# A two-block model on one core: eight more buffers for the modulation weights in S5, y read back by another queue, and three norms whose row factor is applied when a product is read out

## The chip, the cores and the metric

The kernel runs on one core of a Trainium2 chip. The metric is the device time of one execution in microseconds (us), lower is better. The core has five engines that run their own instruction streams and meet at semaphores: PE (TensorE, matmuls), DVE (VectorE), ACT (ScalarE), POOL (GpSimd) and SP (SyncE, here only transfers). ACT and POOL can start transfers too.

## The reference

```python
# first block (512 tokens and 16 meta tokens, width 1024)
n = _rmsnorm(h, g_mix[layer])
proj = n @ w_in[layer]
...
y_ssd = _ssd_mixer(xbc, dt_raw, z, dt_bias[layer], a_log[layer], d_ssd[layer], g_ssd[layer])
y_s5 = _s5_mixer(u, lam_re[layer], lam_im[layer], log_step[layer], ...)
mix = jnp.concatenate([y_ssd.astype(h.dtype), y_s5.astype(h.dtype)], axis=-1)
h = h + mix @ w_out[layer]
m = _rmsnorm(h, g_mlp[layer]) @ w_up[layer]
h = h + jnp.square(jax.nn.relu(m)) @ w_down[layer]
# _ssd_mixer ends with _rmsnorm(y * silu(z), g_norm)
# _s5_mixer ends with _rmsnorm(v[..., :D_S5] * jax.nn.sigmoid(v[..., D_S5:]), g_norm), v = gelu(y) @ w_glu + b_glu
# _rmsnorm(x, g): x * rsqrt(mean(x * x, axis=-1) + 1e-5) * g
```

A second block of two layers follows (convolution, windowed attention, gated merge, convolutional FFN, each modulated by `silu(c) @ w_ada + b_ada`). The change does not touch its code. Only its modulation weights matter here: the kernel computes `silu(c) @ w_ada` piece by piece inside the first block.

## The kernel before, in words

Activations lie transposed: 128 channels on the partitions, tokens along the row, eight tiles of 128 channels. Each fp32 product is made of three products of fp32r halves (hi of the weights by hi of the input, hi by lo, lo by hi). A **unit** is the 128 output channels of one weight tile of 512 KB: 24 matmuls of 512 columns. Its raw weights land in one of R = 4 slots of `wraw`; ACT copies them to `whi` (`split_hi`, L237), POOL subtracts to get `wlo` (`split_lo`, L245), PE multiplies into PSUM bank s, and ACT or DVE reads the bank out and frees it (`acc_free`). Slot s is split again for unit g + 4 as soon as unit g is done. The first four units of a matrix run interleaved as a **quad** (`pe_quad`, L314), so that they can start while the input tiles still come one by one; the others run one after another (`pe_unit`, L284).

The stages in order of time, with their places in the program:

- SSD (`ssd_pe`, `ssd_dve`, `ssd_act`): four chunks of 128 tokens. Its squares are summed over channels by one-column matmuls (`ssd_sums_pe`, L805).
- A norm before a product: ACT squares each tile, DVE adds the squares up (`norm_add`, L412), PE sums over partitions (L446), ACT takes the root, DVE the reciprocal, PE spreads the row over all partitions (`norm_rows_pe`, L454), DVE scales each tile by gain and row factor (L498), ACT rounds it to hi (L437), DVE subtracts to get lo (L508). PE's first matmul of the next quad waits for all that. It happens after SSD, after GLU (norm "s5") and after the second output product (norm "mlp").
- OUT1 (units U_OUT1, eight), added to `res` by `add_unit_dve` (L1022).
- S5: eight passes. In a pass i DVE scans the states (`s5_scan`) and makes tables for pass i + 2 (`s5_tables`), PE forms states and output (`s5_w_pe`, `s5_y_pe`, L1354, L1367, L1375), ACT applies gelu, writes y to memory in eight transfers (L1452), moves the kernel tile in eight more (`s5_move`, L1425) and rounds the y that came back (`s5_hi`, L1429). SP reads y back in another layout (`s5_y_back`, L1239). Between these PE computes the modulation (`ada_pe`, L664), eight tiles of `w_ada` a pass; the tiles land in the four `wraw` slots, so SP can be four ahead, and SP issues in program order: a wait of y's way back holds the weight loads behind it.
- GLU (16 units), OUT2 (8 units), then the MLP: four chunks c, each with 8 up units and 8 down units. For up unit m ACT takes the relu out of PSUM (`rl`, L1524), splits the weights of the unit four later (L237), and rounds the square to `hhi` (L1529); DVE squares (`rv`, L1554) and subtracts (`hlo`, L1556). In the last chunk ACT and DVE also do the squares of the context's norm (L401, L412).

Of the kernel before, what the change touches and what calls it, by code (L numbers as in the profile page):

```python
# [24 lines left out]
P = 128  # L25
# [39 lines left out]
U_ADA = U_GLU + R  # L65
# [54 lines left out]
def build(nc, A, out, ud, yd, pd):  # L120
# [18 lines left out]
    wlo = at("wlo", [P, R, 8, P], 32 * K, F32R)  # L139
    O_H, O_HC, O_X = 48 * K, 64 * K, 72 * K  # L140
# [45 lines left out]
    acc_free = [sem(f"acc_free{s}") for s in range(R)]  # L186
    s_in = [sem(f"inputs_landed{h}") for h in range(4)]
# [119 lines left out]
    def pe_quad(pe, g, i, rb, xh, xl, T, nk=8, hi=None, lo=None, wide=False, c0=0, more=None, between=None, held=None):  # L307
# [347 lines left out]
    def ada_pe(pe, first, last):  # L655

        for u in range(first, last):
            a, j = divmod(u, 12)
            s, rnd = ada_slot(u)
            pe.wait_ge(landed[s], (rnd + 1) * 16)  # L660
            w = wraw[:, s].rearrange("p (k a) m -> p k (a m)", k=2)
# [147 lines left out]
    def ssd_pe(pe):  # L809
# [36 lines left out]
        for c in (NCH - 2, NCH - 1):  # L846
            ssd_sums_pe(pe, c)
# [30 lines left out]
    def ssd_square_act(act, c):  # L878
# [3 lines left out]
        else:  # L882
            act.wait_ge(d_gd.sem, d_gd.past("g"))
        act.activation(xbc[:, 0:NT, chunk(c)], Y[:, :, chunk(c - 1)], ACT.Square).then_inc(d_sq.sem, 1)

    def ssd_act(act):
# [17 lines left out]
        ada_cols(act, 2)  # L904
        ssd_square_act(act, NCH - 1)
# [63 lines left out]
    def ssd_dve(dve):  # L969
# [32 lines left out]
        for g in range(2):  # L1002
# [99 lines left out]
    s_yr = [sem(f"s5_y_landed{b}") for b in range(2)]  # L1102
# [324 lines left out]
    def s5_hi(act, i):  # L1427
        act.wait_ge(s_yr[i % 2], 16 * (i // 2 + 1))
        act.activation(hhi[:, i], yf[:, i % 2], ACT.Copy).then_inc(f_h.sem, 1)  # L1429

    def s5_act(act):
# [4 lines left out]
        for i in range(NT):  # L1436
            if i + 1 < NT:
                s5_move(act, i + 1)
            if i in ADA_END:
                ada_rows(act, ADA_END[i])  # L1440
            if i:
# [7 lines left out]
            if i >= 2:  # L1449
                act.wait_ge(s_yr[i % 2], 16 * (i // 2))  # L1450
# [11 lines left out]
    def glu_act(act):  # L1462
# [4 lines left out]
        for m in range(NT):  # L1467
# [7 lines left out]
            if m:  # L1475
                norm_square(act, n, m - 1, src, SEQ, out_done)
# [1381 lines left out]
```

## Time and profile before

| | |
|---|---|
| median of 3 runs | 3154.59 us (3140.21 to 3154.74) |
| the profiled execution | 3153.16 us |
| its span, first to last instruction | 3151.4 us |
| PE busy | 2870.8 us, 91% of the span |
| DVE busy | 1604.7 us, 51% |
| POOL busy | 1266.5 us, 40% |
| ACT busy | 1086.8 us, 34% |
| mean granted clock of TensorE | 0.958 of full speed |

The span is the profiler's, the time around it is 1.8 us more. Busy times are averages over stages with different limits; what a change is worth is read in its own stage.

### The profile page before, as it was taken

To read this page: it belongs to the slowest core of one execution; us is meant where nothing else is said; L and a number is where in the kernel's file an instruction comes from. 1 tells how busy PE (TensorE), PEld (TensorE's weight loads), DVE (VectorE), ACT (ScalarE), POOL (GpSimd) and SP (SyncE) were. 2 spreads that over 40 slices of the span, in tenths; PEclk is the share of its full clock that TensorE was granted. 3 is DMA by queue.
4 is the path that set the end of the run, shared out by engine and by line. 5 is a ranking of instruction groups with operands and counts; after the bars stand their busy time and mean duration, and the time that the engine had idled before them with its cause. 6 is when DMAs were issued, how large, how long until landed. Compare 5 with 4: busy or idle time off the path is not lost.

```text
span 3151.4 us, 41933 instructions
## 1 busy us (share of the span) xinstructions
PE 2870.8 (91%) x15576; PEld 2323.1 (74%) x15576; DVE 1604.7 (51%) x2055; ACT 1086.8 (34%) x1593; POOL 1266.5 (40%) x689
## 2 busy tenths in 40 slices
PE   6999877989998998988878999999988989799997
PEld 6975634778777887766667888888876767687786
DVE  6864674353334254388854422313246976552424
ACT  4534222323223232235433522313242453253332
POOL 3442200424434181486632322222337773434443
PEclk9989898989999999999989999999989999899999
DMA  5226587323223233422121112111222211222221
GB/s 174 91 80 214 169 251 222 100 74 95 93 79 107 81 121 120 147 76 72 61 67 60 67 60 64 63 61 60 74 81 97 71 61 62 93 80 94 93 92 69
DMA packets 116017, 306.80 MB, mean 97 GB/s; under 512 B 36128, under 2 KB 44448, under 8 KB 115232
## 3 DMA queue, kind: packets, MB, share of 16 engines
q1 hardware_dynamic: 87008, 286.06, 27.8%
q10 hardware_dynamic: 28864, 18.76, 2.2%
q8 instruction: 97, 1.59, 0.2%
q14 instruction: 48, 0.39, 0.0%
HBM read 294.95 MB, written 7.45 MB: 96 GB/s over the span
## 4 chain that ended last, share of the span: by engine, by line
PE 72%; DVE 13%; DVEq 5%; ACT 3%; DMA 2%; issue 2%; ACTq 1%; SPq 1%; POOL 0%; POOLq 0%
PE ps L284 35%; PE ps L314 18%; PE ps L305 6%; DVE co L2043 4%; PE ps L1751 2%; DVEq L2044 2%; PE ps L2154 2%; PE ps L664 1%; DMA wraw<-w_ada 1%; DVE sm L2019 1%; DVE pex L2028 1%; DMA wraw<-stream 1%; DVE mv L2233 1%; PE ps L1755 1%; PE ps L1756 1%
## 5 line engine op out<-in xcount | busy, mean ns | idle before, releaser
L245 POOL TENSOR_TENSOR wlo<-wraw,whi 128x1024 fp32r<-128x1024 f32 x373 | 925.6, 2490 | 1707.5 <-ACT whi L237 1706.0
L237 ACT ACTIVATE whi<-wraw 128x1024 fp32r<-128x1024 f32 x373 | 392.6, 1055 | 554.4 <-PE ps L314 174.5
L284 PE MATMUL ps<-xhi,whi 128*128 128x512 f32 (+1 forms) x1328 | 469.8, 370 | 1.7 <-issue 1.7
L284 PE MATMUL ps<-xlo,whi 128*128 128x512 f32 (+1 forms) x1328 | 470.6, 371 | 0.0
L284 PE MATMUL ps<-xhi,wlo 128*128 128x512 f32 (+1 forms) x1328 | 334.0, 371 | 0.0
L284 PEld LDWEIGHTS ps<-xhi,whi 128*128 128x128 f32 x1328 | 240.5, 188 | 48.1 <-issue 2.7
L284 PEld LDWEIGHTS ps<-xlo,whi 128*128 128x128 f32 x1328 | 240.5, 188 | 44.5
L284 PEld LDWEIGHTS ps<-xhi,wlo 128*128 128x128 f32 x1328 | 232.3, 188 | 44.8
L2043 DVE SCALAR_TENSOR_TENSOR co<-ub,vec,co 128x512 f32<-128x512 f32 (+1 forms) x216 | 251.7, 1205 | 5.4 <-issue 0.4
L1024 DVE SCALAR_TENSOR_TENSOR res<-ps,mod,res 128x512 f32 (+1 forms) x64 | 47.6, 748 | 260.0 <-PE ps L305 151.4
L2140 POOL TENSOR_TENSOR co<-co,ct 128x512 f32<-128x512 f32 (+1 forms) x144 | 164.0, 1139 | 20.7 <-issue 0.4
L284 PE MATMUL ps<-hhi,whi 128*128 128x512 f32 x408 | 159.2, 390 | 2.0 <-DVE gt L2227 1.8
L284 PE MATMUL ps<-hlo,whi 128*128 128x512 f32 x408 | 158.8, 389 | 0.0
L1755 PE MATMUL ps<-xhi,whi 128*128 128x512 f32 x352 | 144.5, 411 | 5.1 <-DVE ub L2055 3.5
L2138 POOL TENSOR_TENSOR ct<-ub,vec 128x512 f32<-128x512 f32 (+1 forms) x144 | 137.0, 951 | 22.9 <-issue 12.6
L2372 DVE SCALAR_TENSOR_TENSOR f<-ps,vec,f 128x511 f32<-128x511 f32 x88 | 50.2, 612 | 176.2 <-ACT f L2344 176.2
L1756 PE MATMUL ps<-xlo,whi 128*128 128x512 f32 x352 | 139.0, 395 | 0.0
L664 PE MATMUL ps<-wraw,cs 128*2 128x512 f32 x384 | 91.3, 620 | 28.8 <-DMA wraw<-w_ada 28.7
L1022 DVE TENSOR_TENSOR res<-res,ps 128x512 f32<-128x512 f32 x48 | 32.7, 687 | 164.4 <-PE ps L314 89.3
L305 PE MATMUL ps<-xchi,whi 128*128 128x256 f32 x352 | 100.5, 286 | 7.3 <-POOL wlo L245 7.3
L314 PE MATMUL ps<-xhi,whi 128*128 128x512 f32 (+1 forms) x320 | 96.5, 402 | 10.3 <-ACT xhi L437 8.8
L314 PE MATMUL ps<-hhi,whi 128*128 128x512 f32 x280 | 91.8, 418 | 14.7 <-DVE fa L2376 6.7
(390 smaller groups left out, 5723.7 us busy)
## 6 DMA issues: line engine op xcount, KB each, us to landing
wraw<-stream SPq DMA_DIRECT2D x425, 512.0 KB, 3.4
wraw<-w_ada SPq DMA_DIRECT2D x96, 512.0 KB, 4.9
biasb<-attn_bias ACTq DMA_DIRECT2D x32, 256.0 KB, 3.2
xin<-x0T SPq DMA_DIRECT2D x4, 528.0 KB, 6.9
s_u<-uk ACTq DMA_DIRECT2D x8, 264.0 KB, 3.4
res<-x0T ACTq DMA_DIRECT2D x1, 2048.0 KB, 8.6
s_y<-yk ACTq DMA_DIRECT2D x64, 32.0 KB, 4.4
yf<-s_y SPq DMA_DIRECT2D x8, 256.0 KB, 2.9
```

Of the source, the lines that this page charges most:

```text
L237: act.activation(whi[:, s], wraw[:, s], ACT.Copy).then_inc(hi_done[s], 1)
L245: pool.tensor_tensor(wlo[:, s], wraw[:, s], whi[:, s].bitcast(F32), ALU.subtract).then_inc(lo_done[s], 1)
L284: last = pe.matmul(ps[:, bank, 0:b - a], w[:, s, kt], x[:, kt, c0 + a:c0 + b], start=start, stop=stop)
L305: return pe.matmul(ps[:, R + s, 0:CTX], w[:, s, kt], part[:, kt], start=start, stop=stop)
L314: last = pe.matmul(ps[:, bank, 0:b - a], w[:, s, kt], x[:, kt, c0 + a:c0 + b], start=start, stop=stop)
L664: ins = pe.matmul(ps[32 * part + 32:32 * part + 34, ada_bank(a), :], cs[:, kt], w[:, h], start=kt == 0, stop=kt == 7)
L1751: last = pe.matmul(o, wraw[:, s, kt], x1[:, kt, 0:p.T], start=kt == 0, stop=kt == NT - 1)
L1755: pe.matmul(o, whi[:, s, kt], xhi[:, kt, 0:p.T], start=kt == 0, stop=False)
L1756: pe.matmul(o, whi[:, s, kt], xlo[:, kt, 0:p.T], start=False, stop=False)
L2043: dve.scalar_tensor_tensor(o, ub[:, m, k:k + p.T], colr(f"dw{p.l}", 1, k * 4 + m), o, ALU.mult, ALU.add)
L2138: pool.tensor_tensor(ct[:, 0:T], ub[:, m, k:k + T], colr(f"dw{l}", 1, k * 4 + m).to_broadcast([P, T]), ALU.mult)
L2140: ins = pool.tensor_tensor(o, o, ct[:, 0:T], ALU.add)
```

## The change

**Buffers.** While S5 runs, `whi` and `wlo` are free. The change lays eight slots `wada` over them, for the modulation tiles from number 40 on, with semaphores of their own; the first round waits for the last OUT1 units. The raw weights of OUT1's second half are loaded before S5's tables instead of after, and those of GLU inside S5, split at its end. **y back** is issued by POOL's queue for passes 0 to 6. **Norms** "ssd", "s5" and "mlp": ACT rounds `src * gain` straight to hi, DVE makes lo, and the row factor multiplies the product when it is read out of PSUM. The sums and the spreading of the row move into the quad. **MLP**: the row factor and the relu are one DVE operation out of PSUM, and ACT squares.

```diff
+RA = 8
+    wada = at("wada", [P, RA, 8, P], 16 * K)
+        if u >= ADA_RAW:
+            return (u - ADA_RAW) % RA, (u - ADA_RAW) // RA
...
         for kt in range(tail):
+            if early and kt == 3:
+                early()
             if hi is not None:
                 hi(pe, kt)
...
+        if between:
+            between()
         for j in range(R):
             product(j, wlo, xh, tail - 1)
...
+    def raw_hi_act(act, n, kt, src, g, dst):
+        act.activation(dst[:, kt, 0:SEQ], src(kt), ACT.Copy, scale=g(kt)).then_inc(n_hi.sem, 1)
+    def raw_row_dve(dve, n):
+        r = norm_row_dve(dve, n, SEQ)
+        dve.tensor_copy(nrs[:, 0:SEQ], r)
+        dve.drain()
+        return nrs[:, 0:SEQ]
+    def raw_lo_dve(dve, n, kt, src, g, hi, lo):
+        dve.wait_ge(n_hi.sem, n_hi.past("hi", hi_before[n] + kt))
+        dve.scalar_tensor_tensor(lo[:, kt, 0:SEQ], src(kt), g(kt), hi[:, kt, 0:SEQ].bitcast(F32), ALU.mult, ALU.subtract).then_inc(n_lo.sem, 1)
...
-        pe.wait_ge(d_wm.sem, d_wm.past("wm", 2 * (NCH - 2)))
-        for c in (1, 2):
-            ssd_sums_pe(pe, c)
         for g in range(2):
             ssd_y_pe(pe, NCH - 1, g)
         ada_turn(pe, 2)
-        for c in (NCH - 2, NCH - 1):
-            ssd_sums_pe(pe, c)
...
+        if r is not None:
+            dve.tensor_tensor(ps[:, s, 0:T], ps[:, s, 0:T], r, ALU.mult)
+            dve.drain()
         d = dst[:, m, 0:T]
...
+            if i == NT - 1:
+                for g in range(U_GLU, U_GLU + R):
+                    split_hi(act, g)
             if i:
                 s5_hi(act, i - 1)
...
+    def out2_act(act):
+        n = NORM["mlp"]
+        added = lambda e, kt: e.wait_ge(acc_free[(U_OUT2 + kt) % R], read_out(U_OUT2 + kt))
+        for m in range(NT):
+            split_hi(act, U_OUT2 + m + R)
+            if m:
+                norm_square(act, n, m - 1, rsrc, SEQ, added)
+        s, rnd = slot(U_OUT2 + NT - 1)
+        act.wait_ge(unit_done[s], rnd + 2)
+        for kt in range(NT):
+            added(act, kt)
+            raw_hi_act(act, n, kt, rsrc, g1("g_mlp"), xhi)
...
+    def raw_pe(pe, U, n, xh, xl, sums):
+        pe_quad(pe, U, 0, 0, xh, xl, SEQ, early=sums, between=lambda: norm_rows_pe(pe, NORM[n], SEQ), **normed(n))
...
# mlp_act, up unit m
-                act.wait_ge(unit_done[s], rnd + 2)
-                act.wait_ge(m_v.sem, m_v.past("v", c * 8 + m, 2))
-                ins = act.activation(rl[:, m % 2], ps[:, s, :], ACT.Relu)
-                ins.then_inc(acc_free[s], 1)
+                act.wait_ge(acc_free[(U_FF + m) % R], read_out(U_FF + m, c, 4))
+                act.wait_ge(m_l.sem, m_l.past("lo", c * 8 + m, 2))
+                act.activation(rv[:, m % 2], rl[:, m % 2], ACT.Square).then_inc(m_v.sem, 1)
                 split_hi(act, U_FF + m + R, c, 4)
                 act.wait_ge(m_v.sem, m_v.past("v", c * 8 + m))
                 act.activation(hhi[:, m], rv[:, m % 2], ACT.Copy).then_inc(m_h.sem, 1)
...
# mlp_dve, up unit m
-                dve.wait_ge(acc_free[(U_FF + m) % R], read_out(U_FF + m, c, 4))
-                dve.wait_ge(m_h.sem, m_h.past("hi", c * 8 + m, 2))
-                dve.tensor_tensor(rv[:, m % 2], rl[:, m % 2], rl[:, m % 2], ALU.mult).then_inc(m_v.sem, 1)
+                dve.wait_ge(unit_done[s], rnd + 2)
+                dve.wait_ge(m_v.sem, m_v.past("v", c * 8 + m, 2))
+                dve.scalar_tensor_tensor(rl[:, m % 2], ps[:, s, :], 0.0, r, ALU.max, ALU.mult).then_inc(acc_free[s], 1)
                 dve.wait_ge(m_h.sem, m_h.past("hi", c * 8 + m))
                 dve.tensor_tensor(hlo[:, m], rv[:, m % 2], hhi[:, m].bitcast(F32), ALU.subtract).then_inc(m_l.sem, 1)
-                if c is LAST:
-                    norm_add(dve, first, m, CTX)
+                for kt in (2 * m, 2 * m + 1) if c is LAST and m < 4 else ():
+                    norm_add(dve, first, kt, CTX)
...
# SP
+            segment(U_OUT1 + R, U_OUT1 + R, R)
...
             for i in range(NT):
                 a = ADA_SSD + ADA_HEAD + 8 * i
                 for j in range(8):
                     if i + 1 < NT:
                         load_ada(a + j)
-                    if j == 1 and i:
-                        s5_y_back(sp, i - 1)
                     if j == 3 and i + 2 < NT:
                         s5_load(sp, i + 2)
+                if i == NT - 3:
+                    segment(U_GLU, U_GLU, R)
             s5_y_back(sp, NT - 1)
...
# POOL
-            pool_units(pool, U_OUT1, 2)
+            pool_units(pool, U_OUT1, 1)
+            for i in range(NT - 1):
+                s5_y_back(pool, i)
+            for g in range(U_GLU, U_GLU + R):
+                split_lo(pool, g)
```

How the order moves at two places. First DVE at the start of the MLP. Before:

```order
L508 SCALAR_TENSOR_TENSOR xlo<-ntt,xhi 128x512 [waits norm_hi] x2
...
L1554 TENSOR_TENSOR rv<-rl 128x512 [waits mlp_hi]
L1555 REGISTER_ALU
L1556 TENSOR_TENSOR hlo<-rv,hhi 128x512 [waits mlp_hi]
L1553 REGISTER_ALU [waits acc_free2]
L1554 TENSOR_TENSOR rv<-rl 128x512 [waits mlp_hi]
```

and now:

```order
L468 SCALAR_TENSOR_TENSOR xlo<-res,vec,xhi 128x512 [waits norm_hi] x8
L427 TENSOR_TENSOR nacc<-nacc,nsq 128x512 [waits norm_square]
L501 RECIPROCAL nst<-nst 128x4 [waits norm_root]
L461 COPY nrs<-ps 128x512 [waits norm_row]
...
L1649 SCALAR_TENSOR_TENSOR rl<-ps,nrs 128x512 [waits mlp_square]
L1650 REGISTER_ALU
L1651 TENSOR_TENSOR hlo<-rv,hhi 128x512 [waits mlp_hi]
L1648 REGISTER_ALU [waits unit_done2]
L1649 SCALAR_TENSOR_TENSOR rl<-ps,nrs 128x512 [waits mlp_square]
```

The reading of a bank (`rl` out of `ps`) now stands on DVE, between the subtraction of one unit and that of the next; before, it was ACT's.

Second SP's transfers in one S5 pass. Before:

```order
L2486 DMA wraw<-w_ada 128x1024 [waits w_lo1]
L2486 DMA wraw<-w_ada 128x1024 [waits w_lo2]
L1239 DMA yf<-s_y 128x512 [waits s5_y_written1]
L2486 DMA wraw<-w_ada 128x1024 [waits w_lo3]
L2486 DMA wraw<-w_ada 128x1024 [waits w_lo0]
L1232 DMA u3a<-s_u 16x8x66 [waits s5_output]
```

and now:

```order
L2590 DMA wada<-w_ada 128x1024 [waits ada_used0]
L2590 DMA wada<-w_ada 128x1024 [waits ada_used1]
L2590 DMA wada<-w_ada 128x1024 [waits ada_used2]
L2590 DMA wada<-w_ada 128x1024 [waits ada_used3]
L1270 DMA u3a<-s_u 16x8x66 [waits s5_output]
L1270 DMA u3a<-s_u 16x8x66 x7
L2590 DMA wada<-w_ada 128x1024 [waits ada_used4]
```

The load of y (`yf`) is gone from SP, and a weight load waits for a slot used eight tiles ago (`ada_used`), not four (`w_lo`).

## Rows read from the trace of the kernel before

**Rows 1.** The page, part 4: the chain that ended last, by engine

```profile
PE 72%; DVE 13%; DVEq 5%; ACT 3%; DMA 2%; issue 2%; ACTq 1%; SPq 1%; POOL 0%; POOLq 0%
```

**Rows 2.** Chain of waits, 600 to 830 us: start us, us, what

```profile
599.81 26.08 PE ps L284 x115
...
633.79 2.09 PE ps L454 x8
...
637.37 25.26 PE ps L314 x96
662.63 22.14 PE ps L284 x96
...
695.93 25.02 PE ps L314 x96
...
744.70 21.39 PE ps L314 x93
```

**Rows 3.** Windows: busy of PE, PEld, DVE, ACT, POOL; clock, DMA share, GB/s

```profile
400.00:524.00 124.00, 95.34 (x1288) 46.28 (x1285) 86.74 (x145) 32.09 (x53) 0.00 (x0) 0.92 0.94 269
...
638.00:644.00 6.00, 6.00 (x17) 4.72 (x16) 5.54 (x10) 2.69 (x5) 0.00 (x0) 0.54 0.00 0
```

**Rows 4.** Timeline of ACT, first MLP chunk: start us, us, line, operation, tiles

```profile
716.22 0.60 ACT L1524 ACTIVATE rl<-ps 128x512 f32<-128x512 f32 x1 [11.04 <-PE ps L314]
716.72 1.05 ACT L237 ACTIVATE whi<-wraw 128x1024 fp32r<-128x1024 f32 x1
717.69 0.63 ACT L1529 ACTIVATE hhi<-rv 128x512 fp32r<-128x512 f32 x1
...
743.60 1.05 ACT L237 ACTIVATE whi<-wraw 128x1024 fp32r<-128x1024 f32 x1
```

**Rows 5.** Timeline of DVE, first MLP chunk

```profile
742.83 2.10 DVE L1556 TENSOR_TENSOR hlo<-rv,hhi 128x512 fp32r<-128x512 f32 x1 [0.70 <-ACT hhi L1529]
...
762.95 0.69 DVE L1022 TENSOR_TENSOR res<-res,ps 128x512 f32<-128x512 f32 x1 [0.90 <-PE ps L314]
```

**Rows 6.** Timeline of POOL, first MLP chunk

```profile
741.71 2.67 POOL L245 TENSOR_TENSOR wlo<-wraw,whi 128x1024 fp32r<-128x1024 f32 x1 [2.72 <-ACT whi L237]
...
762.56 9.48 POOL L245 TENSOR_TENSOR wlo<-wraw,whi 128x1024 fp32r<-128x1024 f32 x4 [15.37 <-ACT whi L237]
```

**Rows 7.** The page, part 5: a product with one PSUM source on DVE

```profile
L1024 DVE SCALAR_TENSOR_TENSOR res<-ps,mod,res 128x512 f32 (+1 forms) x64 | 47.6, 748 | 260.0 <-PE ps L305 151.4
```

**Rows 8.** Timeline of ACT, last MLP chunk, first unit read

```profile
985.64 0.60 ACT L1524 ACTIVATE rl<-ps 128x512 f32<-128x512 f32 x1 [17.03 <-PE ps L314]
```

**Rows 9.** Chain of waits, 0 to 1600 us: norm after SSD, last down quad

```profile
320.53 2.09 PE ps L454 x8
324.11 24.59 PE ps L314 x96
...
1021.91 23.77 PE ps L314 x96
```

**Rows 10.** Waits, 374 to 532 us: who for whom, us in total, times, longest

```profile
PE ps L1334 <- DVE res L1022: 4.2, 1, 4.2
```

**Rows 11.** Timeline of PE in S5, passes 0 and 6

```profile
397.19 1.16 PE L1367 MATMUL ps<-spv,cab 64*64 64x64 f32 x64
...
513.00 1.16 PE L1367 MATMUL ps<-spv,cab 64*64 64x64 f32 x64
```

**Rows 12.** Timeline of ACT in S5

```profile
455.14 5.42 ACTq L1425 DMA_DIRECT2D mt<-ka  x8
...
471.20 5.79 ACTq L1425 DMA_DIRECT2D mt<-ka  x8
...
478.99 0.63 ACT L1429 ACTIVATE hhi<-yf 128x512 fp32r<-128x512 f32 x1
```

**Rows 13.** Timeline of SP in S5: y read back

```profile
471.77 0.33 SPq L1239 DMA_DIRECT2D yf<-s_y  x1
```

**Rows 14.** The page, part 6: y's way back, us to landing

```profile
yf<-s_y SPq DMA_DIRECT2D x8, 256.0 KB, 2.9
```

More of the change, by code:

```diff
@@ L186, in build @@
     acc_free = [sem(f"acc_free{s}") for s in range(R)]
+    ada_landed = [sem(f"ada_landed{s}") for s in range(RA)]
+    ada_used = [sem(f"ada_used{s}") for s in range(RA)]
     s_in = [sem(f"inputs_landed{h}") for h in range(4)]
@@ L196, in raw_round @@
     def raw_round(g, i=0, rb=0):
-        return slot(g, i, rb)[1] + (N_ADA // R if g >= U_ADA else ADA_SSD // R if g >= U_OUT1 + R else 0)
+        return slot(g, i, rb)[1] + (ADA_RAW // R if g >= U_GLU else ADA_SSD // R if g >= U_OUT1 + R else 0)
     def whole(g):
@@ L212, in ada_slot, with ada_worked @@
     def ada_slot(u):
-        return slot(U_ADA + u if u >= ADA_SSD else U_OUT1 + R + u)
+        if u >= ADA_RAW:
+            return (u - ADA_RAW) % RA, (u - ADA_RAW) // RA
+        return slot(U_GLU + u if u >= ADA_SSD else U_OUT1 + R + u)
+    def ada_worked(eng, u):
+        s, rnd = ada_slot(u)
+        eng.wait_ge((lo_done if u < ADA_RAW else ada_used)[s], rnd + 1)
     def loop(eng, n, body):
@@ L305, in second, with pe_quad @@
         return pe.matmul(ps[:, R + s, 0:CTX], w[:, s, kt], part[:, kt], start=start, stop=stop)
-    def pe_quad(pe, g, i, rb, xh, xl, T, nk=8, hi=None, lo=None, wide=False, c0=0, more=None, between=None, held=None):
+    def pe_quad(pe, g, i, rb, xh, xl, T, nk=8, hi=None, lo=None, wide=False, c0=0, more=None, between=None, held=None, early=None):
         tail = nk - 2
@@ L516, in build @@
             "c1a": 9, "l1a": 10, "l1b": 11, "final2": 12}
-    hi_before, lo_before, done, kept_lo = [], [], 0, 0
+    RAW = ("ssd", "s5", "mlp")
+    hi_before, lo_before, t_before, done, kept_lo, scaled_done = [], [], [], 0, 0, 0
     for name in NORM:
+        t_before.append(scaled_done)
+        scaled_done += 0 if "final" in name or name in RAW else NT
         hi_before.append(done)
@@ L804, in ssd_sums_pe @@
         for kt in range(NT):
-            last = pe.matmul(ps[:, 0, c - 1:c], xbc[:, kt, chunk(c)], ones[:, 0:1], start=kt == 0, stop=kt == NT - 1)
+            last = pe.matmul(ps[:, 4, c - 1:c], xbc[:, kt, chunk(c)], ones[:, 0:1], start=kt == 0, stop=kt == NT - 1)
         if c == NCH - 1:
@@ L1005, in ssd_dve @@
             y = Y[:, 4 * g:4 * g + 4, chunk(c - 1)]
-            ins = dve.tensor_tensor(y, y, zs[:, 4 * g:4 * g + 4, chunk(c - 1)], ALU.mult)
-        ins.then_inc(d_gd.sem, 1)
+            dve.tensor_tensor(y, y, zs[:, 4 * g:4 * g + 4, chunk(c - 1)], ALU.mult).then_inc(d_gd.sem, 1)
         dve.drain()
+        for kt in range(NT):
+            raw_lo_dve(dve, NORM["ssd"], kt, ysrc, g1("g_ssd"), hhi, hlo)
     ysrc = lambda kt: Y[:, kt]
@@ L1101, in build @@
     s_yw = [sem(f"s5_y_written{b}") for b in range(2)]
-    s_yr = [sem(f"s5_y_landed{b}") for b in range(2)]
+    s_yr = [sem(f"s5_y_landed{i}") for i in range(NT)]
     e_pa, e_pv = steps("s5_param_scalar", "step", "mag", "sin"), steps("s5_param_vector", "ls", "angle", "kept")
@@ L1558, in chunk @@
                     dve.drain()
-                if c is LAST:
-                    norm_add(dve, first, m, CTX)
+                for kt in (2 * m, 2 * m + 1) if c is LAST and m < 4 else ():
+                    norm_add(dve, first, kt, CTX)
             if c is not LAST:
@@ L2498, in _ @@
                 s5_load(sp, i)
-            segment(U_OUT1 + R, U_OUT1 + R, U_ADA - U_OUT1 - R)
-            for u in range(ADA_SSD, ADA_SSD + ADA_HEAD):
+            for u in range(ADA_SSD, ADA_RAW):
                 load_ada(u)
@@ L2531, in _ @@
             ssd_pe(pe)
[L2532 to L2533 removed]
+            raw_pe(pe, U_OUT1, "ssd", hhi, hlo, lambda: raw_sums_ssd(pe))
             s5_pe(pe)
```

141 lines of the change are left out of this document (90 added, 51 removed).

## Prediction

> **What bounds the kernel now.** I read the page first, then the chain of waits, then the timelines of the stages that the change touches. PE holds 72% of the chain [rows 1], so a change counts where it moves PE's next matmul. In the chain PE stands still at each norm: GLU's last matmul ends at 625.9, the row is spread at 633.8, OUT2's quad starts at 637.4 and ends at 662.6 [rows 2]; OUT2 ends at 684.8, the MLP's quad runs from 695.9 to 720.95 [rows 2]. [...] So a quad after a stop takes 25.3 or 25.0 us, while 93 matmuls took 21.4 at 744.7 [rows 2], which is 22.1 for 96: the stop costs another 3.1 us. In S5 the passes take (513.00 - 397.19) / 6 = 19.3 us [rows 11] with the DMA engines 0.94 busy [rows 3]. In the MLP almost nothing is idle: the down quad starts at 744.7, 0.05 us after ACT's split of the last weights ended at 744.65 [rows 2, 4].
>
> **The change, part by part.** Negative is time won, in the profiled execution.
>
> *Norm after SSD.* The sums of the squares move behind the last products, into the quad. PE's work is the same, only short gaps go, such as the 1.5 us from 322.6 to 324.1 [rows 9]; the long row of one-column sums now lies inside the quad, where the clock may fall again. Nothing to -5 (the gap, another like it, and the quad's 24.6 against 22.1) [rows 9]; I take -2.
>
> *Before S5.* PE waited 4.2 us for DVE, which had tables to make ahead of the last adds [rows 10]. POOL now splits only four units there instead of eight, so the tables are done early; left is the last bank's read, now a product and an add of 0.69 each, 1.5 with the hand-over [rows 5]. 1.5 - 4.2 = -2.7, between -4 and -1.
>
> *S5.* Two floors. ACT's own work of a pass, with no one late, took 471.20 - 455.14 = 16.1 us [rows 12]. The transfers: 124 us at a share of 0.94 are 117 us of work over 124 / 19.3 = 6.4 passes, so 18.1 us a pass [rows 3, 11], less what the eight added slots bring in before pass 0. GLU's four tiles come in on top. I take 17.3, so 6 x (17.3 - 19.3) = -12; the ends are 16.1 (-19) and 19.3 (0). y back by POOL's queue has no row. y's way back starts at 471.77 and lands 2.9 later, and ACT uses it at 478.99 [rows 12 to 14]: it may come 4.3 us later at no cost. Its own price I take as nothing, its ends are nothing and the rival below. Its gain is that SP's loads no longer queue behind it, which is in the 17.3.
>
> *End of S5.* ACT splits GLU's four units just before the last pass: 4 x 1.05 = 4.2 us [rows 4], mostly while it waits for PE. POOL's four need 4 x 2.4 [rows 6] and end before the quad wants them. Nothing to +4; I take +1.
>
> *Norm "s5".* PE can start the quad when GLU's last two banks are read (a sigmoid like the relu's 0.60 [rows 4] and a strided product, longer than 0.75 [rows 7]): some 2 us after 625.9, of which the first matmuls fill 0.5. Then 22.1 for the quad and, inside it, sums and row, 2.1 each at most at half clock [rows 2], say 3 together. 1.5 + 22.1 + 3 = 26.6 against 662.6 - 625.9 = 36.7: -10. Should the clock still fall, -7; at best -12.
>
> *Norm "mlp".* ACT may write `xhi` only after OUT2's last unit: its split 1.05, a square, a hi of 0.63 [rows 4], 2.3 us. The first lo needs DVE, whose add of squares is held by POOL's split (see below) until 1.05 + 2.67 + 0.55 = 4.3, then 0.7: about 5 us [rows 4 to 6], of which four matmuls fill 1. So 4 + 22.1 + 3 + 3.1 for the clock = 32.2 against 36.2 [rows 2]: -4, between -8 and -1.
>
> *The MLP's chunks.* This is the large term. DVE now reads the bank, waits for ACT's square, split and hi, subtracts, and only then reads the next bank. One round: read 0.75 [rows 7], to the split 0.50, to hi 0.97, hi 0.63 [rows 4], hand-overs 0.1: the subtraction starts at 2.95. ACT's split ended at 2.35 and POOL's started. The trace shows what that does: the subtraction at 742.83 ran into POOL's 741.71 to 744.38 and ended at 744.93, 0.55 after it [rows 5, 6]; the add out of PSUM at 762.95 ran in 0.69 beside POOL's row from 762.56 [rows 5, 6]. So operations with both sources in SBUF wait for POOL's end, those out of PSUM do not. POOL ends at 2.4 + 2.4 to 2.67, the subtraction at about 5.5: one unit costs 5.5 us. The four units of the quad finish 1.6 apart and the others 5.5 apart (22.14 / 4 [rows 2]), so the lag of the quad is never made up: unit 7 is read 7 x 5.5 = 38.5 after unit 0, and its weights' slot is split 2.4 later, at 716.2 + 40.9 = 757.1 against 744.65 before [rows 4]. PE's down quad cannot bring in its fourth unit before that: +12.4, and 3.1 for the clock after the stop. Three chunks: +46.5. In the last one the adds of the context's squares come two a unit in the first four, some 0.85 us a unit more (two of half the width of 0.69, with their drain): 4 x 6.35 + 3 x 5.5 + 2.4 = 44.3 after 985.6 [rows 8] is 1029.9 against 1021.9 [rows 9]: +8, and the quad 25.1 instead of 23.8: +9.3. Together +55.8. The alternative reading of the same row is that the subtraction takes a fixed 2.1 us beside POOL, so 5.1 a unit: 3 x (9.6 + 3.1) + 6.5 = +44.6. I take the first and keep 44 and 65 as ends.
>
> [...]
>
> Sum: -2 - 2.7 - 12 + 1 - 10 - 4 + 55.8 = **+26**. 3153.2 + 26 = **3179 us**. The profiled execution stands 1.4 us under the median of the runs, so that against the median it is +25, 0.8% slower.
>
> **The rivals.**
>
> *The MLP's chain is quick enough.* If nothing holds DVE's subtraction, a unit costs 2.95 + 0.69 = 3.65, unit 7 is read on time (7 x 3.65 = 25.6, PE needs 26.9), and the last chunk even wins some 5. Then -30 - 5: 3118 us. For it: ACT's square relieves DVE of one held operation of the two. Against: POOL's split starts before the subtraction in every unit. The point is 3.8 us a unit; above it, PE waits. Chance 0.12.
>
> *The chain costs less than I say*: 5.1 a unit, 3168 us, within no change. For it: the rows of 2.1. Against: the ends tied to POOL's. Chance 0.13.
>
> *S5 wins nothing.* y comes back more than 4.3 us late through POOL's queue and ACT waits for it ahead of the gelu, or the DMA engines are the limit at 19.3 after all. In front of y's use DVE runs its tables; if POOL cannot issue during them (12 operations of about 0.69 each [rows 5], some 8 us, less the 4.3 of slack), y is 4 late and the pass is 16.1 + 4 = 20. Then +38 to +42: 3191 to 3195. Against: POOL has nothing else to do in S5. [...] Chance 0.15.
>
> **How the numbers follow.** My own case has 0.60 and, with its ends (44 to 65 for the MLP, the smaller terms partly offset), runs from 3165 to 3200. The range 3140 to 3202 takes in the middle rival and the S5 rival and leaves out the fast one (0.12) and a tail above. A measurement of this kernel can tell some 0.5%, 15.8 us, from no change: 3139 to 3170. Faster: the first rival and a sliver, 0.13. Within: the second rival and the low end of my case, 0.17. Slower: 0.70.
>
> **What would show it.** Right: in every MLP chunk about 12 us between the last up unit and the main part of the down quad, with PE waiting for ACT's `whi`; the subtraction of `hlo` near 2.4 us and starting 5.5 apart; half clock at the start of the down quads; S5 passes near 17.3; OUT2's quad starting within 2 us of GLU's end. Wrong: up units read 4 us apart or less, no idle PE before the down quads, or S5 passes of 19 and more with ACT waiting for y.

## Result and profile after

| | before | after |
|---|---|---|
| median | 3147.7 us (6 runs, 3140.21 to 3154.74) | 3174.27 us (6 runs, 3166.6 to 3180.37) |
| ratio | | 1.0085, 95% interval 1.007 to 1.010 |
| profiled execution | 3153.16 us | 3171.6 us |
| its span | 3151.4 us | 3169.8 us |
| mean granted clock | 0.958 | 0.955 |

The change costs 26.6 us by the medians and 18.4 us between the two spans. The forecast was 3179 us, slower. In the page's chain, PE's share has fallen from 72% to 68% and "issue" has risen from 2% to 7% [rows 1]:

```profile
PE 68%; DVE 14%; issue 7%; DVEq 5%; ACT 3%; DMA 1%; ACTq 1%; POOL 0%; SPq 0%; POOLq 0%
```

The chain of waits of after, 600 to 830 us (start, length, what), answers to [rows 2]:

```profile
612.92 7.16 PE ps L325 x30
620.09 0.79 PE ps L477 x8
620.87 8.46 PE ps L325 x36
629.33 0.89 PE ps L485 x8
630.22 6.47 PE ps L325 x28
636.69 22.14 PE ps L295 x96
...
660.59 2.38 DVE nacc L427
663.06 0.76 DVE xlo L468
663.87 8.92 PE ps L325 x28
...
706.35 0.70 DVE rl L1649
...
723.47 1.05 ACT whi L248
724.56 23.96 PE ps L325 x93
748.52 21.77 PE ps L295 x96
771.43 16.95 PE ps L325 x72
```

To read the losses and gains, take the same event in both traces and follow the difference from one to the next. GLU's end: 625.9 before, 610.8 now, so 15 us are won up to there. OUT2's quad ends at 636.69 instead of 662.63: 25.9 won. It starts 2.1 us after GLU's end and its sums (0.79) and row (0.89) stand inside it. The MLP's first quad ends at 689.4 instead of 720.95: 31.6 won, the most there ever is. From there it is lost again. The first down quad's main part starts at 724.56 instead of 744.70 (20.1 won), and so on through four chunks, until behind the last down quad the changed kernel is 14.7 us late. The second block gives the other 3.6 us: its code is the same, and one of its operations took 1247 ns on average instead of 1205 (L2138, 216 times, 9.1 us in all), and what sets that is open. Of the eleven runs below six have 1233 to 1247 ns there and five 1200 to 1214, so up to 10 us of DVE's work in a single trace belong to no change under test.

Where the MLP loses can be seen on DVE and POOL. Timelines of after, 700 to 722 us, DVE and then POOL:

```profile
698.46 2.48 DVE L1651 TENSOR_TENSOR hlo<-rv,hhi 128x512 fp32r<-128x512 f32 x1 [2.17 <-ACT hhi L1621]
700.86 0.68 DVE L1649 SCALAR_TENSOR_TENSOR rl<-ps,nrs 128x512 f32<-128x512 f32 x1
703.71 2.48 DVE L1651 TENSOR_TENSOR hlo<-rv,hhi 128x512 fp32r<-128x512 f32 x1 [2.17 <-ACT hhi L1621]
706.35 0.69 DVE L1649 SCALAR_TENSOR_TENSOR rl<-ps,nrs 128x512 f32<-128x512 f32 x1 [0.16 <-issue]
```

```profile
697.98 2.41 POOL L256 TENSOR_TENSOR wlo<-wraw,whi 128x1024 fp32r<-128x1024 f32 x1 [3.09 <-ACT whi L248]
703.23 2.40 POOL L256 TENSOR_TENSOR wlo<-wraw,whi 128x1024 fp32r<-128x1024 f32 x1 [2.84 <-ACT whi L248]
```

Each subtraction of `hlo` starts 0.47 or 0.48 us after POOL's split has begun and ends 0.54 to 0.56 us after the split has ended (703.23 + 2.40 = 705.63, 703.71 + 2.48 = 706.19). The next bank is read after it. The page has all 32 of them:

```profile
L1651 DVE TENSOR_TENSOR hlo<-rv,hhi 128x512 fp32r<-128x512 f32 x32 | 78.6, 2457 | 69.8 <-ACT hhi L1621 69.8
```

In the first chunk the banks are read at 684.69 and, seven units on, at 722.22: 5.36 us a unit. From the end of its first up unit to that of its last PE computes for only 26.9 us of the 37.5, so it stands still before the down quad and then begins it at a granted clock of 0.50. Windows of after (busy of PE, PEld, DVE, ACT, POOL; clock, DMA share, GB/s):

```profile
724.00:728.00 4.00, 3.44 (x8) 2.76 (x9) 2.44 (x1) 1.03 (x2) 2.36 (x1) 0.50 0.21 85
728.00:740.00 12.00, 12.00 (x50) 9.76 (x50) 0.00 (x0) 0.00 (x0) 0.00 (x0) 0.91 0.13 44
```

In S5 the passes took (494.89 - 387.25) / 6 = 17.9 us instead of 19.3 [rows 11]; the timeline of PE in passes 0 and 6:

```profile
387.25 1.16 PE L1405 MATMUL ps<-spv,cab 64*64 64x64 f32 x64
...
494.89 1.16 PE L1405 MATMUL ps<-spv,cab 64*64 64x64 f32 x64 [0.59 <-DVE spv L1341]
```

A new wait appears there. In the waits, 370 to 530 us, PE hardly waits for modulation weights any more, but ACT waits for y (us in all, times, longest):

```profile
ACT hhi L1467 <- DMA yf<-s_y: 32.0, 5, 11.9
...
PE ps L701 <- DMA wada<-w_ada: 1.2, 2, 0.8
```

Of the same window before, the rows are

```profile
PE ps L664 <- DMA wraw<-w_ada: 26.1, 18, 3.4
...
ACT hhi L1429 <- DMA yf<-s_y: 1.9, 1, 1.9
```

### The profile page after: what moved, and what is told of

The parts are those of the page before. It is cut to its first block, busy times and chain, and to the rows that moved or that the text cites. A ratio compares the mean times of both kernels' runs of the same rounds, so it can differ in the third digit from the quotient of the medians.

```text
span 3169.8 us, 41861 instructions
## 1 busy us (share of the span) xinstructions
PE 2866.9 (90%) x15576; PEld 2317.3 (73%) x15576; DVE 1596.6 (50%) x2050; ACT 1086.1 (34%) x1593; POOL 1260.2 (40%) x696
## 4 chain that ended last, share of the span: by engine, by line
PE 68%; DVE 14%; issue 7%; DVEq 5%; ACT 3%; DMA 1%; ACTq 1%; POOL 0%; SPq 0%; POOLq 0%
PE ps L295 34%; PE ps L325 17%; PE ps L316 6%; DVE co L2138 4%; PE ps L1846 2%; DVEq L2139 2%; PE ps L2249 2%; DVE sm L2114 1%; DVE hlo L1651 1%; DVE mv L2328 1%; DMA wraw<-stream 1%; DVE pex L2123 1%; PE ps L701 1%; ACT whi L248 1%; DVE rl L1649 1%
## 5 line engine op out<-in xcount | busy, mean ns | idle before, releaser
L256 POOL TENSOR_TENSOR wlo<-wraw,whi 128x1024 fp32r<-128x1024 f32 x373 | 915.0, 2461 | 1576.8 <-ACT whi L248 1575.4
L295 PE MATMUL ps<-xhi,whi 128*128 128x512 f32 (+1 forms) x1328 | 469.8, 370 | 1.7 <-issue 1.7
L2138 DVE SCALAR_TENSOR_TENSOR co<-ub,vec,co 128x512 f32<-128x512 f32 (+1 forms) x216 | 260.8, 1247 | 5.4 <-issue 0.5
L325 PEld LDWEIGHTS ps<-hhi,whi 128*128 128x128 f32 x280 | 58.6, 211 | 79.2 <-ACT whi L248 61.2
L1651 DVE TENSOR_TENSOR hlo<-rv,hhi 128x512 fp32r<-128x512 f32 x32 | 78.6, 2457 | 69.8 <-ACT hhi L1621 69.8
```

What stands on the lines that cost most here:

```text
L256: pool.tensor_tensor(wlo[:, s], wraw[:, s], whi[:, s].bitcast(F32), ALU.subtract).then_inc(lo_done[s], 1)
L295: last = pe.matmul(ps[:, bank, 0:b - a], w[:, s, kt], x[:, kt, c0 + a:c0 + b], start=start, stop=stop)
L325: last = pe.matmul(ps[:, bank, 0:b - a], w[:, s, kt], x[:, kt, c0 + a:c0 + b], start=start, stop=stop)
L1651: dve.tensor_tensor(hlo[:, m], rv[:, m % 2], hhi[:, m].bitcast(F32), ALU.subtract).then_inc(m_l.sem, 1)
L2138: dve.scalar_tensor_tensor(o, ub[:, m, k:k + p.T], colr(f"dw{p.l}", 1, k * 4 + m), o, ALU.mult, ALU.add)
```

## Experiments

Eleven runs of ten kernels, each beside runs of the kernel before on its own chip. Ratios are to it; the change itself has 1.0085.

**The MLP: which part of the unit's round holds PE?** The theory is the prediction's: read, square, hi and the held subtraction stand one behind the other. The rival was that the new norm as such costs time.

*Subtraction one unit behind.*

```diff
# mlp_dve, unit m, behind the read of the bank; low(c, m) holds what is taken out
-                dve.wait_ge(m_h.sem, m_h.past("hi", c * 8 + m))
-                dve.tensor_tensor(hlo[:, m], rv[:, m % 2], hhi[:, m].bitcast(F32), ALU.subtract).then_inc(m_l.sem, 1)
+                if m:
+                    low(c, m - 1)
+            low(c, 7)
```

> The changed kernel, but in the MLP DVE subtracts hlo of up unit m only after it has read bank m + 1 out, so that its reads wait for nothing of ACT or POOL. Chain theory (a read of 5.4 us a unit is what holds the down quad): the 11.5 us of idle PE before each down quad go, the MLP takes about 46 us less than in the changed kernel, and the run is near 3127 us, 0.7 per cent under the kernel before. Rival (the row factor on DVE and the square on ACT cost this wherever they stand in the order): no difference from the changed kernel, about 3174 us.

Measured 3120.66 us (3117.04 to 3127.55), ratio 0.9911 (0.9883 to 0.9938); again on another chip:

> The version with the subtraction one unit behind once more, in five rounds and on the chip of the two others: 3117 to 3125 us, 0.9 to 1.1% under the kernel before, passes of 17.5 to 18.3 us in S5.

3115.11 us (3110.58 to 3128.72), ratio 0.9890 (0.9869 to 0.9912). That is some 6 us better than I expected the first time, and 2 us under the range the second. The timeline of DVE shows reads 5.5 us apart only where PE finishes units that slowly. The hold itself mostly stays: the median of the 32 subtractions is still 2.3 us, as in the first line below, and the reads around that one are 3.7 us apart (690.68, 694.41). What is gone from the round is DVE's wait for ACT's square, split and rounding between the read and the subtraction. Once POOL has caught up, a subtraction meets it idle and takes 0.68 us:

```profile
692.00 2.48 DVE L1646 TENSOR_TENSOR hlo<-rv,hhi 128x512 fp32r<-128x512 f32 x1 [0.63 <-ACT hhi L1621]
...
704.86 0.69 DVE L1657 SCALAR_TENSOR_TENSOR rl<-ps,nrs 128x512 f32<-128x512 f32 x1 [1.92 <-PE ps L295]
705.47 0.68 DVE L1646 TENSOR_TENSOR hlo<-rv,hhi 128x512 fp32r<-128x512 f32 x1
```

Its window 690 to 1090, and that of after, show what PE got back (1482 matmul records against 1725, and the clock):

```profile
690.00:1090.00 400.00, 390.15 (x1725) 319.99 (x1724) 132.37 (x155) 116.97 (x170) 169.14 (x91) 1.00 0.32 97
```

```profile
690.00:1090.00 400.00, 350.29 (x1482) 282.85 (x1481) 130.39 (x120) 106.28 (x146) 140.61 (x59) 0.93 0.26 79
```

*Hi ahead of the split.*

```diff
# mlp_act, unit m
-                split_hi(act, U_FF + m + R, c, 4)
                 act.wait_ge(m_v.sem, m_v.past("v", c * 8 + m))
                 act.activation(hhi[:, m], rv[:, m % 2], ACT.Copy).then_inc(m_h.sem, 1)
+                split_hi(act, U_FF + m + R, c, 4)
```

"Lock theory" stands for the prediction's reading of [rows 5, 6]: a subtraction that begins during POOL's split is held until the split has ended (there it ended 0.55 us after it).

> The changed kernel, but ACT rounds hhi of an up unit before it splits the next weights, so that the subtraction mostly starts before POOL's split; DVE's order stays as changed. Lock theory: subtractions of 0.69 us instead of 2.46 in most units, reads about 3 to 3.5 us apart where they lag, nothing idle before the down quads, near 3128 us. Rival (a serial order costs by itself, whatever POOL does): reads still 5 us apart, 3160 us or more.

Measured 3130.49 us (3124.43 to 3135.30), ratio 0.9938 (0.9917 to 0.9959). Here DVE's order is that of the change, with the same data, the same read and the same wait for hi. Two things move: hi comes earlier (the subtraction starts 2.06 us after the read, not 2.85), and POOL's split starts later, because ACT's does. Timelines of DVE and POOL:

```profile
698.78 1.30 DVE L1651 TENSOR_TENSOR hlo<-rv,hhi 128x512 fp32r<-128x512 f32 x1 [1.36 <-ACT hhi L1620]
...
702.30 0.69 DVE L1651 TENSOR_TENSOR hlo<-rv,hhi 128x512 fp32r<-128x512 f32 x1 [1.36 <-ACT hhi L1620]
703.61 0.69 DVE L1649 SCALAR_TENSOR_TENSOR rl<-ps,nrs 128x512 f32<-128x512 f32 x1 [0.62 <-PE ps L295]
```

```profile
697.12 2.42 POOL L256 TENSOR_TENSOR wlo<-wraw,whi 128x1024 fp32r<-128x1024 f32 x1 [0.95 <-ACT whi L248]
699.78 2.58 POOL L256 TENSOR_TENSOR wlo<-wraw,whi 128x1024 fp32r<-128x1024 f32 x1 [0.24 <-ACT whi L248]
703.30 2.40 POOL L256 TENSOR_TENSOR wlo<-wraw,whi 128x1024 fp32r<-128x1024 f32 x1 [0.94 <-ACT whi L248]
```

The subtraction at 702.30 starts as one split ends, is over before the next, and takes 0.69 us instead of 2.48; units are read 703.61 - 700.24 = 3.4 us apart. So it is in 24 of the 32. The other eight start late in a split and take 1.21 to 1.30 us: the one at 698.78 starts 1.66 us into the split and still ends 0.54 us after it (697.12 + 2.42 = 699.54, 698.78 + 1.30 = 700.08). The end is tied to POOL's, wherever the subtraction starts. That is a wait, not a fixed slowing. This is the prediction's first rival (3.65 us, nothing held) made by hand, and the down quad's main part starts 3 us after the last up unit instead of 13. Hi's 0.8 us alone would not have done it: 2.06 + 2.48 is 4.5 us a unit, over the 3.8.

*Both.*

> The changed kernel with both repairs of the MLP's order at once: DVE subtracts for unit m - 1 after it has read unit m, and ACT rounds hi ahead of the split of the weights. Each alone gave 3120.7 and 3130.5 us. Theory chain: neither leaves PE waiting for a split once a unit costs under 3.8 us, so what is left of the two differences is in the handing over to the down quad; both together come out at 3117 to 3121, no better than the first alone by more than 3 us. Rival: each removes a cost of its own (about 53 and 44 us), and the second adds a few microseconds more, because hi is there one split (1.05 us) earlier in each of the last units of four chunks: 3113 to 3117.

Measured 3124.07 us (3111.22 to 3126.86), ratio 0.9903 (0.9875 to 0.9931): the intervals of this and of the first repair overlap almost wholly, so no gain of the second on top can be seen; the median lies above both ranges that I had given. In its chain the down quad starts 3.0 us after the last up unit (714.06 to 717.10), with the first repair alone 2.4 (715.88 to 718.26): with hi first, the split that PE needs next comes one rounding later.

**What each half of the change is worth.** *The change with the MLP and its norm as before*: `RAW` without "mlp", the functions `mlp_pe`, `mlp_act` and `mlp_dve` of before, and the norm's tiles scaled before the quad as before.

```diff
-    RAW = ("ssd", "s5", "mlp")
+    RAW = ("ssd", "s5")
```

> The changed kernel with the norm ahead of the MLP and the MLP's own order as they were before the change. Chain theory: 46 us won in the MLP's chunks, 5.6 lost at its norm, near 3133 us, 0.5 to 0.7 per cent under the kernel before. Rival (the loss is spread over the other stages): above 3150 us.

Measured 3128.41 us (3120.47 to 3136.07), ratio 0.9937 (0.9916 to 0.9958): everything but the MLP wins 20 us. *The kernel before with the MLP and its norm alone as in the change*:

```diff
+    RAW = ("mlp",)
```

> The kernel before with only the norm ahead of the MLP and the MLP's order as changed. Chain theory: 46 us lost in the chunks, 5.6 won at the norm: 40 us or 1.3 per cent slower than before. Rival (the loss comes from how the parts meet): within 10 us of the kernel before.

Measured 3190.04 us (3187.47 to 3192.38), ratio 1.0131 (1.0107 to 1.0154), so 41 us lost, and the page's row is that of the change to a nanosecond:

```profile
L1614 DVE TENSOR_TENSOR hlo<-rv,hhi 128x512 fp32r<-128x512 f32 x32 | 78.6, 2456 | 69.7 <-ACT hhi L1584 69.7
```

-20 and +41 give +21; the whole change has +27. The halves add up within their intervals (some 6 us to either side of the first).

**S5: why does y come late?** Two theories: POOL's queue is slow by itself, or the weight loads in flight share the DMA engines with y (depth).

*y by SP again, behind two weight loads.*

```diff
# SP, pass i
                         load_ada(a + j)
+                    if j == 1 and i:
+                        s5_y_back(sp, i - 1)
...
# POOL
-            for i in range(NT - 1):
-                s5_y_back(pool, i)
```

> The changed kernel with y read back by SP again, behind two weight loads of its pass, for passes 0 to 6; all else as changed. In the changed kernel y lands 5.6 us after its issue by POOL's queue (2.9 before), ACT waits for it and a pass takes 17.9 us. Theory POOL's queue (the load itself is slow because POOL's queue carries it): y's load takes 3 to 3.5 us again once issued, but SP stands between it and weight loads that now wait for slots used eight tiles ago, so it is issued up to 2 us later; passes 16.5 to 17.5, the kernel 3 to 10 us faster than changed (3164 to 3171). Theory depth (eight weight loads of 512 KB in flight share the DMA engines with it, whatever the queue): y lands 5 us or more after its issue here too, behind SP's loads, and passes take 18 to 19.5 us: 3174 to 3186.

Measured 3183.36 us (3181.17 to 3190.67), ratio 1.0103 (1.0085 to 1.0121), passes (517.00 - 396.34) / 6 = 20.1 us. Neither theory had it: the time lies in the range of depth, which had y landing after 5 us or more, but y lands 2.6 us after its issue. PE waits for weights as before the change; waits, 370 to 530 us:

```profile
PE ps L701 <- DMA wada<-w_ada: 24.8, 12, 3.6
```

SP stands at y's wait with only two loads of the pass given out, and the slots that come free meanwhile stay empty.

*Four slots instead of eight*, y on POOL's queue:

```diff
-RA = 8
+RA = 4
```

> The changed kernel with four modulation slots in the ring in place of eight; y stays on POOL's queue. Theory depth: half as many weight loads are in flight, y lands in 3 to 4 us, ACT hardly waits for it, but PE waits for weights again as before (some 25 to 35 us over S5): passes 18 to 19.3 us, the kernel 3174 to 3183. Theory POOL's queue: y still lands in 5.6 us or more, ACT waits for it as much as in the changed kernel, and PE waits for weights on top: passes 19.3 or more, 3182 to 3190.

Measured 3179.12 us (3172.32 to 3181.77), ratio 1.0084 (1.0064 to 1.0105), passes (509.26 - 387.10) / 6 = 20.4 us, with

```profile
PE ps L701 <- DMA wada<-w_ada: 26.6, 12, 4.0
...
ACT hhi L1467 <- DMA yf<-s_y: 1.8, 1, 1.8
```

ACT hardly waits for y, as depth said, but y still took 5.2 us to land (5.6 with eight slots, both over 380 to 520 us), as the queue theory said: the wait had moved to PE, and hid the landing. How much eight slots are worth is less clear than these passes look. The profiled execution was the slowest of four, as that of the variant above was, and the ratio is the change's own.

*y by ACT's queue.*

```diff
# s5_move of pass i + 1, before its sixth transfer
+            if k == 5 and back is not None:
+                s5_y_back(act, back)
```

> The changed kernel with y of the pass before read back by ACT's queue, issued between the fifth and the sixth of ACT's eight transfers of the kernel tile. Theory POOL's queue: it lands in about 3 us and is there before ACT's gelu is over; ACT's 28 us of waits for y go, what is left is ACT's own work of 16.1 us a pass or the transfers' 17: passes 16.3 to 17.3, the kernel 4 to 11 us faster than changed (3163 to 3170). Theory depth: it lands in 5.6 us or more also from here, ACT waits 3 to 4 us a pass for it, passes 18 us and the kernel at 3172 to 3178.

Measured 3182.13 us (3175.98 to 3190.62), ratio 1.0107 (1.0079 to 1.0134), passes (498.64 - 381.29) / 6 = 19.6 us. Depth had 3172 to 3178 us and passes of 18; the time is above that, but not the one that a slow queue of POOL's would give (3163 to 3170). y lands 6.4 us after its issue, up to 10.1 (tile `yf`, 370 to 540 us):

```profile
DMA to landing us min/median/max: 2.6/6.4/10.1
```

and ACT waits 32.4 us for it, as with POOL's queue. So POOL's queue has no slowness of its own that ACT's doesn't have.

*Six slots*, on top of the MLP with the subtraction one unit behind:

```diff
-RA = 8
+RA = 6
```

> The version with the subtraction one unit behind (3120.7 us), with six modulation slots in place of eight, y on POOL's queue. With eight slots ACT waits for y some 25 to 32 us over S5 and PE hardly for weights; with four slots ACT hardly waits for y and PE 27 us for weights; passes of 17.9 and 20.4 us. Theory depth: six slots lie between, y lands in about 5 us, PE's waits for weights and ACT's for y are both 5 to 15 us; passes 17 to 18.5 us, the kernel 3115 to 3124. Rival: the transfers are the floor whatever the depth, and any slot fewer only costs: passes 18.5 to 19.5, 3124 to 3130.

Measured 3115.57 us (3109.38 to 3121.50), ratio 0.9887 (0.9868 to 0.9906), passes (491.90 - 381.61) / 6 = 18.4 us, ACT 29.9 us behind y, PE 4.4 behind weights: no different from eight slots, run beside it (0.9890). The time is inside the range of the depth theory, but what it names isn't there: y took longer to land (7.1 us), not shorter.

*y by SP, behind six weight loads*, eight slots, the same MLP, and POOL's loop taken out:

```diff
+                    if j == 5 and i:
+                        s5_y_back(sp, i - 1)
```

> The version with the subtraction one unit behind, eight slots, y read back by SP again but behind six of the eight weight loads of its pass, where behind two gave passes of 20.1 us. Theory order: SP then stands at y's wait with six loads already given out, so PE has its weights; y follows them in the same queue and lands 5 to 8 us after its issue, ACT waits as with POOL's queue: passes 17.5 to 18.5, the kernel 3117 to 3126. Rival: y comes so late behind the loads (each 512 KB, 48 of them in 112 us, 2.3 us apiece) that ACT waits 6 us or more in a pass: passes 20 or more, 3132 to 3140.

Measured 3112.12 us (3105.47 to 3115.18), ratio 0.9871 (0.9851 to 0.9891), passes (496.54 - 390.38) / 6 = 17.7 us, and

```profile
ACT hhi L1467 <- DMA yf<-s_y: 22.1, 4, 7.3
...
DMA to landing us min/median/max: 2.5/2.9/3.9
```

y lands as fast as before the change with eight slots in use, so the 5 to 8 us I expected of loads ahead of it in the same queue did not come, and the time is below the 3117 to 3126 that went with them. What differs from POOL's and ACT's queue is that SP, which issues the weight loads, gives out none while it stands at y's wait. It doesn't save as much as it seems: ACT's eight writes of y took longer to land. Medians of 380 to 520 us, out (`s_y`) and back (`yf`): 4.7 and 3.2 before, 3.8 and 5.6 after, 3.7 and 4.6 in the second run of the first repair, 3.7 and 6.4 by ACT's queue, 5.6 and 2.9 here. Both ways together are 7.9 us before and 8.3 to 10.1 in these four. With the DMA engines 0.91 to 0.97 busy over 388 to 500 us in all five, the queue seems to decide mainly on which leg y waits. That is read off these medians, not tested by itself. This version has the lowest median of all, though its interval overlaps that of the same MLP with y on POOL's queue.

*What the single loads show.* Take each load of y issued between 375 and 535 us by itself, with the busy share of the DMA engines over the 3 us behind its issue, y's own part included. In the twelve traces other than that of the kernel before with the new MLP, 44 loads had a share of 0.82 or less and landed in 2.5 to 5.6 us, median 2.9; 40 had more and landed in 3.4 to 10.1, median 7.0. POOL's loads alone do the same (24 with a median of 3.0, 32 with 7.4). Whether DVE is at its tables matters little beside that. In the run with both repairs POOL issued one at 446.15, with DVE idle from the end of its tables until 453.19, and it took 6.4 us; in the one with the old MLP it issued one at 472.90 amid the tables, and it took 3.3. Windows of the two, 3 us each (DVE busy 0.00 and 2.85, DMA share 1.28 and 0.82):

```profile
446.15:449.15 3.00, 3.00 (x15) 1.23 (x14) 0.00 (x0) 0.00 (x0) 0.54 (x1) 0.52 1.28 206
```

```profile
472.90:475.90 3.00, 3.00 (x33) 0.83 (x31) 2.85 (x6) 0.00 (x0) 0.54 (x1) 0.50 0.82 190
```

So what makes y late, in the main, are the loads beside it, as depth said, and not the queue that issues it. This is a comparison within traces; no run changed the traffic alone.

**How far one trace fixes S5.** After, each repair, both together, the second run of the first and the change with the old MLP have the same code up to OUT2, yet pass 0 of S5 begins anywhere from 380.48 to 391.78 us, OUT2's quad ends from 631.96 to 641.14, and passes are 17.5 to 18.3 us. So one trace fixes the stage to some 5 us. What the runs of S5 show beyond that is where the waits lie and how long y takes to land. Of their times, the ratios tell only that neither the queue of y nor the number of slots was worth more than some 10 us: 1.0084 to 1.0107 round the change's 1.0085, and 0.9871 to 0.9890 with the repaired MLP.

## Why the prediction was right

The sum was +26 us; it measured +26.6 by the medians and +18.4 in the profiled executions. The profiled execution of before is 5.5 us above the median of its six runs, that of after 2.7 below its own: that is the 8 us between the two. The sum was made for the profiled execution and is 7.6 us too high there; that it meets the medians so closely is luck. The terms' own misses are -9.5 to +3.6 us and partly cancel. Term by term, predicted and measured in the traces:

| term | predicted | measured |
|---|---|---|
| norm after SSD | -2 | -5.4 |
| before S5 | -2.7 | -2.9 |
| six passes of S5, with its start | -12 | -9.8 |
| end of S5 | +1 | +3.6 |
| norm "s5", with 0.5 in GLU | -10 | -11.4 |
| norm "mlp" | -4 | -5.7 |
| MLP chunks | +55.8 | +46.3 |
| second block | 0 | +3.6 |

- **The MLP's chain was right, its sum 9.5 too large.** A unit cost 5.36 us, not 5.5: from the read to the subtraction 2.84 to 2.95, predicted 2.95, and the subtraction ends 0.55 after POOL's end, as predicted. Three parts of it were mis-sized by about 3 us each. PE came 11.4 us late to each of the first three down quads (predicted 12.4). The clock's part was 2.6, 1.9 and 1.6, where I took 3.1 for each from the quads after a norm (93 matmuls in 23.96, 23.31 and 22.95 against 21.4 before; granted clock 0.89, 0.91 and 0.93 over them against 1.00, and 0.88 and 0.89 over the two quads after a norm). In the last chunk the down quad started 6.9 us late instead of 8, and it had been slow already: I had it 1.3 us longer, and it got 0.9 shorter (96 matmuls in 23.77 before, 93 in 22.89 now). Chunk by chunk 14.0, 13.3, 13.0 and 6.0.
- **Held or only slowed.** The rival with 5.1 a unit lies 0.26 below, my 5.5 lies 0.14 above the measured 5.36. In the changed kernel every subtraction starts at the same point of the split, so its end alone does not tell a wait from a fixed slowing. What decides is the repair with hi first: started later in the split, a subtraction takes 1.2 to 1.3 us and ends as long after POOL as ever, and 0.69 where POOL is idle. So 2.48, 1.30 and 0.69 us are one operation with more, less and nothing to wait for. The forecast's choice of 5.5 over 5.1 had only the one row for it (742.83, ending 0.55 us after POOL's split [rows 5, 6]). What ties the two ends is not shown.
- **Quick enough** (3118 us, 0.12) did not happen, but both repairs produce it, at 3115 to 3130 us. Its condition, under 3.8 us a unit, held.
- **S5.** Passes of 17.9 against 17.3. The step that failed is "its own price I take as nothing": y landed 5.6 us after its issue instead of 3.2 (both over 380 to 520 us; 2.9 on the page before [rows 14]), up to 8.1, and ACT waited 28 to 32 us for it in four or five waits. The rival "S5 wins nothing" put it at 4 us a pass and 20 us; the longest waits were longer than that (11.9), but passes remained well under 20, since before the change the same passes had lost 26 us on PE to the weights, which are gone. So its mechanism was there, and its price wasn't in this trace. By the medians it isn't excluded: all but the MLP wins 20 us there, and the terms before S5 and the norm "s5" make 5.4 + 2.9 + 11.4 = 19.7 of it, which leaves S5 about nothing, where the traces have -9.8 and +3.6. How much S5 gained stays open within these 6 us or so. As the cause it supposed that POOL might not be able to issue during DVE's tables, which no row showed. The runs speak against that: by ACT's queue y took as long to land (6.4 us), and by POOL's 6.4 us with DVE idle and 3.3 amid the tables.
- **End of S5.** +3.6 instead of +1, and most of it is y's lateness again. The last pass begins 512.34 - 494.89 = 17.45 us after pass 6, where it was 527.74 - 513.00 = 14.74. That is 2.7 of the 3.6, and ACT's splits had not begun. ACT came to the rounding of y late and waited 1.06 us there, which held DVE's scan. Timelines of ACT and, below, PE:

```profile
505.33 0.63 ACT L1467 ACTIVATE hhi<-yf 128x512 fp32r<-128x512 f32 x1 [1.06 <-DMA yf<-s_y]
...
512.41 3.90 ACT L248 ACTIVATE whi<-wraw 128x1024 fp32r<-128x1024 f32 x4
516.21 0.61 ACT L1467 ACTIVATE hhi<-yf 128x512 fp32r<-128x512 f32 x1
516.85 0.60 ACT L1487 ACTIVATE yk<-ps 128x512 f32<-128x512 f32 x1
```

```profile
514.25 1.97 PE L1413 MATMUL ps<-u3a,mt 128*64 128x64 f32 x32
```

The four splits took 3.90 us and the rounding follows them without a gap, but the gelu behind it (`yk`) needs PE's output, which ended at 516.22. The gelu started 0.6 us after that, and at once before the change. So the splits cost about 0.6, within the +1.
- **Norms.** Both near: OUT2's quad starts 2.1 us after GLU's end ("within 2" was foretold), and the clock did not fall in it: the window 638 to 644, at 0.54 before [rows 3], reads

```profile
638.00:644.00 6.00, 6.00 (x28) 4.89 (x27) 4.96 (x6) 1.95 (x3) 6.00 (x4) 1.00 0.65 219
```

After SSD more was won than the -2 I took, at the end of its range (0 to -5). With the one-column sums inside the quad the clock came down, as feared: 0.98 over 310.00 to 316.00, then 0.74 over 316.00 to 325.20. Chain of after:

```profile
306.90 9.09 PE ps L325 x32
316.00 9.27 PE ps L841 x64
325.26 10.92 PE ps L325 x36
```

36 matmuls took 10.92 us there (clock 0.75 over 325.30 to 336.20) and 8.46 in OUT2's quad (1.00 over 620 to 630). It won all the same. The likely reason is that the last products of SSD no longer stood behind such a row; that is read from the order in the trace, and no run took it apart.

## What to carry to other kernels

Before an operation moves to another engine, write out one full round with the holds in it, and compare it with the time that PE takes for a unit: 5.4 against 5.5 us looks even, yet the four units of a quad finish within 5 us (716.2 to 720.95 before), and a round over 3.8 us never makes that up. When a DVE operation meets a POOL operation each time and is held by it, as `hlo`'s subtraction was by the split (2.46 us on average, 0.69 with POOL idle), it can be enough to shift one of the two, and nothing has to be removed: either so that they no longer meet (hi first), or so that the held operation no longer stands between a wait and the read that PE needs (subtraction one unit behind, where most are still held, median 2.3 us). The change as a whole lost 27 us, and the same change with one subtraction moved behind the next read wins 28 to 35 (ratios 1.0085 against 0.9911 and 0.9890, and 0.9871 with y back on SP behind six loads).

A larger ring of buffers took away PE's waits for weights (26 us to 1) only where the queue that fills it didn't stand at another wait: with SP behind y after two loads they were back at 25 us, after six at 4.5. What it won there, ACT lost on y (32.0 us of waits against 1.9), which shared the DMA engines with the loads (0.97 busy over 388 to 500 us). In the runs' times four, six and eight slots can't be told apart.

## What was not expected of the hardware

- The landing of the same 256 KB went with what ran beside it: median 2.9 us where the DMA engines were at most 0.82 busy over the 3 us behind its issue, 7.0 where they were busier. By SP, which gives out no weight load while it waits to issue it, it took 2.5 to 4.4 us; by POOL's queue up to 8.9, by ACT's up to 10.1.
- Quads after a stop of PE did not all pay the same for the clock: 1.6 to 2.6 us in the MLP after waits of PE of at most 4.9 us each with matmuls between, 3.1 after a norm before the change. The granted clock was low at the start of both: 0.54 over 638 to 644 before [rows 3], 0.50 over 724 to 728 and then 0.91 over 728 to 740 in the MLP now. Whether the length of the stop makes the difference wasn't tried.
